# A float32 transformer kernel: the opening's loads and products, and the last gated activations of the convolution and feed-forward stages, put in another order

## What is computed

```python
def first_block(x, ln1_g, w_in, ...):
    h = rmsnorm(x, ln1_g[l])
    z = h @ w_in[l]
    ...
    x = x + mix @ w_out[l]
    h2 = rmsnorm(x, ln2_g[l])
    u = causal_dwconv(h2 @ w_up[l], ffn_conv[l])
    x = x + (jax.nn.silu(u[..., :D_FF]) * u[..., D_FF:]) @ w_down[l]

def _swiglu(x, w_gate, w_up, w_down):
    return (jax.nn.silu(x @ w_gate) * (x @ w_up)) @ w_down

x = _layer_norm(alpha * x + 0.5 * _swiglu(x, ...), ln_gain, ln_bias)
```

## Time and profile before

| | us |
|---|---|
| median of 3 runs | 1390.08 (1389.57 to 1390.72) |
| the profiled execution, its device time | 1389.59 |
| its span, first to last instruction | 1387.8 |
| PE busy | 1367.1 (99% of the span) |
| PE weight loads busy | 1164.4 (84%) |
| DVE busy | 886.2 (64%) |
| ACT busy | 683.1 (49%) |
| POOL busy | 126.3 (9%) |
| mean granted TensorE clock | 0.998 |

### The profile page before, as it was taken

One profiled execution on the slowest core, in us unless ns is written; L12 is line 12 of the kernel. 1 busy time (PEld: TensorE's weight loads), 2 busy tenths in 40 slices (PEclk: granted clock), 3 DMA queues, 4 the chain that ended last, 5 costly groups with the idle time before them and its releaser, 6 DMA issues.

```text
span 1387.8 us, 21095 instructions
## 1 busy us (share of the span) xinstructions
PE 1367.1 (99%) x7520; PEld 1164.4 (84%) x7520; DVE 886.2 (64%) x1280; ACT 683.1 (49%) x1037; POOL 126.3 (9%) x236
## 2 busy tenths in 40 slices
PE   9999999999999999999999999999999999999997
PEld 6988999998888879987888887888879988888885
DVE  5877776675554574688655557555476987855555
ACT  5674655554444435595444444444446753444441
POOL 5431100000000011282000000000000001000000
PEclk9999999999999999999999999999999999999999
DMA  9535965664555547505655564655555434555550
GB/s 309 168 91 164 292 199 182 188 189 150 184 188 190 188 127 224 172 2 167 213 181 181 182 215 151 209 182 184 194 166 183 152 105 138 189 190 190 188 182 30
DMA packets 190086, 242.16 MB, mean 174 GB/s; under 512 B 7824, under 2 KB 171937, under 8 KB 190032
## 3 DMA queue, kind: packets, MB, share of 16 engines
q1 hardware_dynamic: 184448, 226.59, 51.5%
q0 software_dynamic: 5440, 13.81, 3.5%
q10 hardware_dynamic: 144, 1.04, 0.2%
HBM read 238.76 MB, written 1.07 MB: 173 GB/s over the span
## 4 chain that ended last, share of the span: by engine, by line
PE 95%; DVE 2%; ACT 1%; issue 1%; DMA 0%; DVEq 0%; ACTq 0%; POOLq 0%
PE ps L736 21%; PE ps L738 21%; PE ps L737 21%; PE ps L567 6%; PE ps L568 6%; PE ps L569 6%; PE ps L759 2%; PE ps L760 2%; PE ps L766 2%; PE ps L2680 2%; PE ps L912 1%; PE ps L1439 1%; PE ps L712 1%; PE ps L1450 1%; DVE wlo L546 1%
## 5 line engine op out<-in xcount | busy, mean ns | idle before, releaser
L562 DVE TENSOR_TENSOR wlo<-raw,whi 128x1024 fp32r<-128x1024 f32 x270 | 323.2, 1223 | 128.3 <-ACT whi L554 128.3
L554 ACT ACTIVATE whi<-raw 128x1024 fp32r<-128x1024 f32 x270 | 276.8, 1055 | 124.1 <-PE ps L738 100.3
L736 PE MATMUL ps<-whi,ahi 128*128 128x512 f32 x792 | 313.7, 396 | 0.8 <-DVE wlo L546 0.8
L738 PE MATMUL ps<-wlo,ahi 128*128 128x512 f32 x792 | 309.3, 390 | 0.0
L737 PE MATMUL ps<-whi,alo 128*128 128x512 f32 x792 | 308.6, 390 | 0.0
L546 DVE TENSOR_TENSOR wlo<-raw,whi 128x1024 fp32r<-128x1024 f32 x142 | 169.7, 1226 | 35.9 <-ACT whi L536 35.4
L567 PE MATMUL ps<-ahi,whi 128*128 128x256 f32 x624 | 177.5, 285 | 0.2 <-ACT arena L2752 0.2
L568 PE MATMUL ps<-alo,whi 128*128 128x256 f32 x624 | 176.5, 283 | 0.0
L569 PE MATMUL ps<-ahi,wlo 128*128 128x256 f32 x624 | 176.5, 283 | 0.0
L736 PEld LDWEIGHTS ps<-whi,ahi 128*128 128x128 f32 x792 | 148.8, 188 | 31.9 <-DVE wlo L546 1.6
L738 PEld LDWEIGHTS ps<-wlo,ahi 128*128 128x128 f32 x792 | 148.7, 188 | 31.5
(11 more groups left out here) (422 smaller groups left out, 1799.9 us busy)
## 6 DMA issues: line engine op xcount, KB each, us to landing
raw<-ffn_w_gate SPq DMA_DIRECT2D x88, 512.0 KB, 3.9
raw<-ffn_w_up SPq DMA_DIRECT2D x88, 512.0 KB, 4.6
raw<-ffn_w_down SPq DMA_DIRECT2D x88, 512.0 KB, 4.2
raw<-w_up SPq DMA_DIRECT2D x44, 512.0 KB, 4.7
raw<-w_down SPq DMA_DIRECT2D x22, 512.0 KB, 4.4
raw<-w_in SPq DMA_DIRECT2D x16, 512.0 KB, 6.3
raw<-nsa_w_in SPq DMA_DIRECT2D x8, 1024.0 KB, 5.7
raw<-hgrn_w_in SPq DMA_DIRECT2D x16, 512.0 KB, 4.6
```

Of the source, the lines that this page charges most:

```text
L554: act.activation(split_half(w_slots(slot)[0], mode), raw_half(h), ACT.Copy).then_inc(hi_ready, 1)
L562: dve.tensor_tensor(lo, raw_half(h), hi.bitcast(F32), ALU.subtract).then_inc(lo_ready, 1)
L736: pe.matmul(dst, a_h, w_h, start=first, stop=False, skip_group_check=True)
L738: return pe.matmul(dst, a_h, w_l, start=False, stop=last, skip_group_check=True)
```

## The change

It does four things.

- **Loads.** The identity and the first gain (one row of 4 KB, not spread) are now issued on ACT's queue, ahead of its table load. x's second tile is loaded after two weight halves, not four. POOL issues three of its small loads before the first `rstd` and the gate weights before the second.
- **Gain.** PE spreads the gain to 128 partitions by two float32 products of one row (512 columns each) into PSUM banks 6 and 7; DVE reads it from there. The zero matmuls are 10 ahead, 3 between and 4 behind the transposes, where there were 16 and 12, and the 8 between the tiles go.
- **Products by parts.** The first 48 matmuls are cut into runs of four: `first_highs` waits for the high weights and high activations only, `first_low_activations` for `alo`, `first_low_weights` for `wlo`. The transposes of tile 1 stand between runs of tile 0, and tile 1's first run stands before tile 0's last.
- **Own buffers at stage ends.** The last gated activations of the convolution stage go to `conv_ghi`, `conv_glo`, those of a feed-forward stage to `last_ghi`, `last_glo`. `high` of the convolution's last step waits no more for PE's earlier product, and DVE's `low` moves ahead of a weight split. In `pe_ffn` each `turn` moves up by one `down` of six matmuls, the `e` products of tile 0 and gate and up of tile 1 with it; all `e` products take the low parts last.

```diff
+        conv_ghi, conv_glo = (nc.alloc_sbuf_tensor_at(name, [P, 2, T], F32R, offset=xc_at + 2048 * n)
+                              for n, name in enumerate(("conv_ghi", "conv_glo")))
+        last_ghi, last_glo = (nc.alloc_sbuf_tensor_at(name, [P, 2, T], F32R, offset=ffn_at + 2048 * n)
+                              for n, name in enumerate(("last_ghi", "last_glo"), 1))
...
-            def down(at, a, m, ends=False):
+            def down(a, m):
                 for x in range(2):
-                    last = pe_down(pe, at + x, x, a, m, last=ends and x == 1)
+                    last = pe_down(pe, d + x, x, a, m)
                 return last
 
-            e = half0[n + 1] - 2
-            for m in range(2):
-                down(d, 0, m)
+            def last_down(a, m):
+                pe.wait_ge(g_hi, turns + LAST + 1 + a)
+                return pe_down_low_last(pe, half0[n + 1] - 2, a, m, (g_ready, turns + LAST + 1 + a))
+
+            down(0, 0)
             pe.wait_ge(gated_ready, mults + 2 * LAST + 1)
             turn([0])
-            down(d, 1, 0)
-            pe.wait_ge(g_ready, turns + LAST + 1)
-            pe.wait_ge(lo_ready, e + 2)
+            down(0, 1)
+            pe.wait_ge(lo_ready, half0[n + 1])
             for m in range(2):
-                down(e, 0, m, True).then_inc(y_done, 1)
+                last_down(0, m).then_inc(y_done, 1)
             gate_up(h, 1, 1).then_inc(half_done, 2)
-            down(d, 1, 1).then_inc(half_done, 2)
+            down(1, 0)
             pe.wait_ge(gated_ready, mults + 2 * LAST + 2)
             turn([1])
+            down(1, 1).then_inc(half_done, 2)
             if p < 7:
                 pe_turn(pe, p + 1, 0, 0)
-            pe.wait_ge(g_hi, turns + LAST + 2)
-            pe_down_low_last(pe, e, 1, 0, (g_ready, turns + LAST + 2)).then_inc(y_done, 1)
+            last_down(1, 0).then_inc(y_done, 1)
             if p < 7:
                 pe_turn(pe, p + 1, 0, 1)
-            down(e, 1, 1, True).then_inc(half_done, 2)
+            last_down(1, 1).then_inc(half_done, 2)
...
             act_split(act, b)
+            act_split(act, b + 1)
             act.wait_ge(gu_done, firsts + FFN_STEPS)
             act.activation(gate_act[:, 0, :], ps[:, 0, 0:256], ACT.Silu).then_inc(silu_ready, 1)
-            act_split(act, b + 1)
-            turned((0,), turns + LAST + 1)
+            turned((0,), turns + LAST + 1, last_ghi)
             act.wait_ge(half_done, body(n, LAST) + 4)
             act.activation(gate_act[:, 1, :], ps[:, 1, 0:256], ACT.Silu).then_inc(silu_ready, 1)
             act_split(act, b + 2)
-            turned((1,), turns + LAST + 2)
+            turned((1,), turns + LAST + 2, last_ghi)
+            act_split(act, b + 3)
             if p < 7:
-                act_turned(act, p + 1, 0, 0)
-                act_split(act, b + 3)
-                act_turned(act, p + 1, 0, 1)
+                for h in range(2):
+                    act_turned(act, p + 1, 0, h)
...
             dve_z_stats(dve, p + 1, 1, 0)
+            dve_z_stats(dve, p + 1, 1, 1)
             if p < 7:
                 dve_turned(dve, p + 1, 0, 1)
-            dve_z_stats(dve, p + 1, 1, 1)
...
             act_split(act, b + 2)
             act_split(act, b + 3)
-            high(FFN_STEPS, body(n, LAST) + 6)
+            high(FFN_STEPS, None, conv_ghi)
...
             taps(1, 2 * LAST + 2, 2 * LAST + 2, last_row)
             product(FFN_STEPS)
             dve_split(dve, b + 2)
+            low(FFN_STEPS, conv_ghi, conv_glo)
             dve_split(dve, b + 3)
...
-            pe_keep_clock(pe, 16)
-            pe.wait_ge(ident_landed, 16)
+            pe_keep_clock(pe, KEEP)
+            pe.wait_ge(ident_landed, 32)
+            for h in range(2):
+                pe.matmul(ps[:, 6 + h, :], ident[0:1, 0:1].to_broadcast([1, P]), gb[0:1, 0, cols_of(h)],
+                          start=True, stop=True).then_inc(gain_spread, 1)
+            pe_keep_clock(pe, 3)
             for h in range(2):
                 pe_turn(pe, 0, 0, h)
-            pe_keep_clock(pe, KEEP)
+            pe_keep_clock(pe, 4)
...
         def act_start(act):
+            act.dma_start(consts[:, 0:N_FIRST], io["shape_constants"][:, 0:N_FIRST]).then_inc(ident_landed, 16)
+            act.dma_start(gb[0:1, 0, :], io["ln1_g"]).then_inc(ident_landed, 16)
             act.wait_ge(zeros_ready, 1)
             act.activation(table_use[:, :], zeros[:, 0:1], ACT.Exp)
             act_square_sum(act, 0)
-            act_turned(act, 0, 0, 0)
             for h in range(2):
                 act_split(act, h)
-            act_turned(act, 0, 0, 1)
+            for h in range(2):
+                act_turned(act, 0, 0, h)
+            act_square_sum(act, 1)
             for h in range(2, 4):
                 act_split(act, h)
-            act_square_sum(act, 1)
-            act_split(act, 4)
             for h in range(2):
                 act_turned(act, 0, 1, h)
             act.dma_start(consts[:, N_FIRST:], io["shape_constants"][:, N_FIRST:]).then_inc(const_landed, 16)
-            act_split(act, 5)
+            for h in range(4, HALF_SLOTS):
+                act_split(act, h)
...
+            def apply(a):
+
+                dve.wait_ge(rstd_ready, a + 1)
+                for h in range(2):
+                    dve.wait_ge(gain_spread, h + 1)
+                    dve.scalar_tensor_tensor(z_tok[:, a, cols_of(h)], x_tok[:, a, cols_of(h)], rstd[:, a:a + 1],
+                                             ps[:, 6 + h, :], ALU.mult, ALU.mult).then_inc(x_ready, 1)
...
+            def first_parts(a, kh):
+
+                w = [w.rearrange("p s (k n) -> p s k n", k=4) for w in w_slots(w_halves[base + 2 * kh][3], 2)]
+                return w, [v[:, 4 * kh:4 * kh + 4, a * P:(a + 1) * P] for v in (ahi, alo)], \
+                    ps[:, a, :].rearrange("p (s n) -> p s n", s=2)
+
+            def first_highs(a, kh):
+                (w_h, _), (a_h, _), dst = first_parts(a, kh)
+                pe.wait_ge(hi_ready, base + 2 * kh + 2)
+                pe.wait_ge(n_hi, tile_half(0, a, kh))
+                for k in range(4):
+                    pe.matmul(dst, a_h[:, k, :], w_h[:, :, k, :], start=kh == 0 and k == 0, stop=False, skip_group_check=True)
+
+            def first_low_activations(a, kh):
+                (w_h, _), (_, a_l), dst = first_parts(a, kh)
+                pe.wait_ge(a_ready, tile_half(0, a, kh))
+                for k in range(4):
+                    pe.matmul(dst, a_l[:, k, :], w_h[:, :, k, :], start=False, stop=False, skip_group_check=True)
+
+            def first_low_weights(a, kh):
+                (_, w_l), (a_h, _), dst = first_parts(a, kh)
+                pe.wait_ge(lo_ready, base + 2 * kh + 2)
+                for k in range(4):
+                    last = pe.matmul(dst, a_h[:, k, :], w_l[:, :, k, :], start=False, stop=kh == 1 and k == 3,
+                                     skip_group_check=True)
+                return last
...
-            for kh in range(2):
-                tokens(0, 0, kh, 0, True)
-            for half in range(2):
-                pe_turn(pe, 0, 1, half)
-            pe_keep_clock(pe, 8)
-            for kh in range(2):
-                tokens(0, 1, kh, 1, True)
+            first_highs(0, 0)
+            first_low_activations(0, 0)
+            first_low_weights(0, 0)
+            pe_turn(pe, 0, 1, 0)
+            first_highs(0, 1)
+            pe_turn(pe, 0, 1, 1)
+            first_low_activations(0, 1)
+            first_highs(1, 0)
+            first_low_weights(0, 1).then_inc(token_tile, 1)
+            first_low_activations(1, 0)
+            first_low_weights(1, 0).then_inc(half_done, 2)
+            first_highs(1, 1)
+            first_low_activations(1, 1)
+            first_low_weights(1, 1).then_inc(half_done, 2)
...
                                     h += 1
-                                    if h == 4:
+                                    if h == 2:
                                         load_x(1)
...
-            pool.wait_ge(ident_landed, 16)
+            for g, row, src in row_sources[:3]:
+                pool.dma_start(rows[row:row + src.shape[0], g, :], src).then_inc(rows_landed, 16)
+            pool.wait_ge(ident_landed, 32)
             pool_rstd(pool, 0, 0)
-            for g, row, src in row_sources:
+            for g, row, src in row_sources[3:]:
                 pool.dma_start(rows[row:row + src.shape[0], g, :], src).then_inc(rows_landed, 16)
             for n, name in ((AQ, "a_q_g"), (AK, "a_k_g")):
                 for twice in range(2):
                     pool.dma_start(rows[n:n + 1, 0, twice * DH:(twice + 1) * DH], io[name]).then_inc(rows_landed, 16)
+            pool.dma_start(gate_w, w_in[:, 1280:1288].rearrange("(k p) n -> p k n", p=P)).then_inc(gate_landed, 16)
             pool_rstd(pool, 0, 1)
```

84 lines of the change are left out of this document (38 added, 46 removed).

## The result

The changed kernel took 1379.11 us (median of six runs, 1377.73 to 1381.13) beside 1389.98 for the kernel before (six runs, 1389.57 to 1390.72). The ratio is 0.9923, with an interval of 0.9911 to 0.9936: 10.9 us faster, where 9.4 were forecast. Five runs more in a later job gave 1380.31 (1378.95 to 1382.17), ratio 0.9929 [0.9915, 0.9942]. So the change is worth about 10 to 11 us, and its eleven single runs are spread over 4.4 us. One run of the kernel before in that later job took 1687.9 us at a granted clock of 0.751 and is left out of every figure.

What follows compares the result with a forecast made beforehand. PE fills 95% of the span, so time is won only where it stands still or works on zeros. 3.4 + 1.7 + 3.8 + 0.5 = 9.4 us off, 1380.2 against the profiled execution, 1380.7 as median; range 1379.3 to 1383.2.

Steps and rivals of the forecast that it cites:

- Opening, 3.4: Kernel start: 49th product at 22.8 instead of 26.40, taken as 3.4 us won; at most 4.2 (22.2), at worst 1.9.
- the row of PE's runs: Opening: PE's order in runs of 0.91 us, from first highs at 10.4 to the 49th product at 22.8.
- TensorE is at its lower level (1.2 GHz) up to about 6.9 us: Opening: half clock until about 6.9 us, 2.4 GHz after, so the gain's two products end near 8.1.
- over long before 5.48: Opening: PE's new wait for identity and gain ends well before the ten zero products do at 5.48 us.
- The 0.97 for one row of 512 columns: Opening: time of one gain product at TensorE's upper level, 0.97 us; 1.94 at the lower.
- The gain's products keep the lower level longer: Opening rival, 11%: clock rises only at 10 us, gain's products end at 9.4, 1.5 us less won, 1382.2.
- x and ACT, weights: Opening loads: x near 4.3 us, weight halves 0 and 1 near 6.8 and 8.2, half 3 near 12.7.
- the sum of 6.4: Total gain in us if, by the skill's rule on queues, the opening's two queues won only 0.44 of issue time.
- Convolution, 1.7: Convolution's end: PE goes on at 311.5 instead of 313.20, 1.7 us won; 1.4 if the low part is late.
- Feed-forward ends, 3.8: Three feed-forward ends before another stage: PE's 1.07 us wait closes and 0.2 is recovered each; 3.8 us, at worst 0.6.
- The rival that the 1.07 stays: Feed-forward ends rival, 10%: PE's 1.07 us wait remains, 3.2 us less won, 1383.9.
- Last end, 0.5: Kernel's last end: PE's 0.47 us wait for `ghi` goes as the `turn` comes 1.4 earlier; 0.5 us won.

Runs made afterwards that it cites:

- maxima_all_again: Repeat run of the changed kernel with the running maxima's four-row float32 products made over 128 rows, the gain's left at one row; 1378.06 us.
- gain_all_rows: Changed kernel with the gain's products over 128 rows, its tile zeroed first (load some 0.5 us later) and 12 zero products ahead instead of 10; 1378.50 us.
- maxima_twice: Changed kernel with the first stage's four-row float32 products of the maxima done twice, 4.0 us in one piece instead of 2.0; 1383.49 us, ratio 0.9942.
- gain_by_dma: Changed kernel with the first gain again spread by a transfer on POOL's queue, PE's two gain products replaced by four of zeros; 1381.14 us, ratio 0.9932.
- both_all_again: Repeat of the changed kernel with gain's and maxima's products over 128 rows, gain tile zeroed first, 12 zero products ahead; 1378.39 us.
- before_maxima_all: The kernel before with only the maxima's four-row products made over 128 rows; 1389.56 us (eleven runs), ratio 0.9996.

## Why the prediction came out as it did

The direction and the places were right. The measured median lies 0.2 below the low end of the range, 1.6 below the point. Of these 1.6, 0.9 is between the two profiled executions, 10.3 apart where the sum was 9.4. The other 0.7 is the step from that execution to the median: I added 0.5, as in the kernel before, and the changed kernel's median lies 0.2 under its profiled execution. With single runs 3.4 us apart that is luck of the draw. The steps, one by one:

- *Opening, 3.4.* This is one of the two terms that were mis-sized: 4.2 in the trace. The step that failed is the row of PE's runs: "highs 14.0; transposes to 15.4; ...: 22.8", with 0.2 more taken off for small gaps. The highs started at 13.46, since tile 1's norm was ready by 12.5 and not at 13.4, and half 3 was split by 13.41 and not 13.8. From there PE needed 8.75 where I had 8.8, and no small gap cost anything: 0.54, 0.05 and 0.2 are the 0.8. The 49th product started at what I had called the least possible, 22.2. The lead lasted through the first stage, as forecast, but for the fall.
- *"TensorE is at its lower level (1.2 GHz) up to about 6.9 us"* was wrong for this execution, but it explains little of the 0.8. I read the moment in one execution and carried it over. Over the eighteen traces the rise came anywhere from 4.1 to 7 us, or, behind few-row products, near 12 to 13. With the rise at 4.3 the gain's products ended at 6.98 and not at 8.1. In maxima_all_again they ended at 7.76, and the 49th product still started at 22.20; in gain_all_rows they ended at 8.14, as forecast, and it started at 22.52, 3.9 ahead. So up to 0.3 of the 0.8 hangs on the rise, and only a rise that comes behind the gain's products costs 3.3. Nor was the wait for gain and identity "over long before 5.48": the products began at 5.00 when the gain landed, and without zeros ahead they could not begin before 4.91. The 0.97 for one row of 512 columns should have been 1.99 / 2, and 0.99 was measured.
- *The gain's products keep the lower level longer*, the rival of 11% at 1382.2, is a state that this opening can be in, not a rival to it: maxima_twice shows it, with the rise near 13 instead of 10 and 3.3 lost instead of 1.5. By that size it fits four of eleven runs of the changed kernel, 1381.1 to 1382.2, though none of the four was traced. I had treated as one outcome for all runs what is drawn anew in each. The Trainium skill, page "TensorE: Matmul & The Clock Gate", section "What's actually happening", has activity lift the rate; no-gap work on one row didn't, in the traces with a 3.78 us row above, while in the two with 2.18 and 2.31 it did not stand in the way.
- *x and ACT, weights.* These came a little earlier than forecast. Half 3 was split at 12.35 (forecast 12.7), halves 0 and 1 at 6.09 and 7.60 (6.8 and 8.2); the norm started 6.69 (7.2). That the queues bring no bandwidth held: the DMA share was 1.07 from 5 to 10 us. But the sum of 6.4 that I drew from the rule of the Trainium skill, page "DMA: Bandwidth & Descriptors", section "Rules for kernel authors", was wrong, since the opening won by what is loaded first and by what isn't loaded at all, as gain_by_dma shows with its 2.0 us.
- *Convolution, 1.7.* 1.75.
- *Feed-forward ends, 3.8.* This is the other term that was mis-sized, by as much: 4.58, 1.53 each instead of 1.27. The mechanism was right, and the wait closed wholly, as forecast. I had taken the idle time that the profile prints, 1.07. From start to start PE lost more: 512.70 plus two products of 0.23 is 513.16, and the transposes start at 514.38, so 1.22; likewise 0.3 and not 0.2 around 504.40 (the two and four small transposes there take 0.85 from 503.99 to 504.84, where six of the kind take 0.54). The rival that the 1.07 stays fell.
- *Last end, 0.5.* 0.76, for the same reason: from start to start PE lost 0.86 before the product at 1376.31 with its two small transposes, which take 0.14 in the changed kernel (1364.64 to 1364.78).
- *The fall behind the maxima's products* was in no step. It took 1.5 in the profile pair, since the trace of before happened to have none, and something under that in the medians, since both kernels have it in part of their runs (by the clock of 0.997, 18 of 44 before and 3 of 11 of the changed one).
- *The 0.4 between 150 and 200 us* came in some kernels and was turned round in others (0.6 lost in gain_by_dma, 0.5 in both_all_again). I didn't test what it hangs on.

So the trace gives 4.2 + 1.75 + 4.6 + 0.8 = 11.3, 11.7 with the 0.4. The kernels without the fall agree: maxima_all_again is 11.5 below before_maxima_all. The measured 10.0 and 10.9 are less than that; late rises in part of the runs would account for it, which these kernels' few traces can't show. The range failed at its low end because I let only the opening go to its best there, and held the ends at a value read from idle times. That the median missed that end by no more than 0.2 is luck: what the ends and the stretch behind 150 us brought beyond it, 1.5 together, the fall took back in the profiled execution.

That the falls behind the maxima's products come from their four rows is shown by the pairs with and without them: five of eleven traces against none of six, and 18 of 44 runs of the kernel before at a clock of 0.997 against none of eleven. For the gain's products it isn't shown. The fall behind them stands in two traces with one or 32 rows and in none of three with 128, while six more with one row, wholly or mostly at the upper level, lack it. The late rise stands in three traces with one row, and in the one pair that differs in the rows alone no run of either kernel is near 1381. Why the chip does either is open.

## What to carry to other kernels

Take a stall's size from start to start of the instructions around it, not from the idle time printed; the difference was a fifth here, three times over. Read the moment at which TensorE rises in several executions before a step is hung on it, give the chances per run, and ask whether the step is on the path at all: rises between 4.1 and 6.2 us moved the 49th product by 0.3 at most, where no fall followed. Where PE must spread a few rows over partitions in one piece, a product over 128 partitions with zeros costs no more time than one over a single row or four, and no trace here has a fall behind it.
